# A Griffin-style decoder block on one Trainium2 core: one projection conversion, the bias conversions and one activation half moved

## What is computed

```python
def mixer(...):
    q, k, v, xr, yr, ga, gl = split_cols(h @ w_in)
    ...
    y_attn = sliding_window_attention(q, k, v, attn_sinks) @ w_attn_o
    ...
    y_lru = (rg_lru(...) * jax.nn.gelu(yr)) @ w_lru_o
    merged = jax.nn.sigmoid(ga) * y_attn + jax.nn.sigmoid(gl) * y_lru
    return merged @ w_out

def moe(...):
    logits = (t @ w_router + b_router).astype(jnp.float32)
    top_val, top_idx = lax.top_k(logits, TOP_K)
    gate = jax.nn.softmax(top_val, axis=-1)
    ...
    def expert_block(args):
        xc, e = args
        gu = xc @ w_gate_up[e] + b_gate_up[e]
        g, u = gu[:, :D_EXPERT], gu[:, D_EXPERT:]
        g = jnp.minimum(g, SWIGLU_LIMIT)
        u = jnp.clip(u, -SWIGLU_LIMIT, SWIGLU_LIMIT)
        act = (u + 1.0) * (g * jax.nn.sigmoid(SWIGLU_ALPHA * g))
        return act @ w_down[e] + b_down[e]
```

## Time and profile before

| | us |
|---|---|
| three runs | 2124.33, 2125.55, 2130.52 |
| median | 2125.55 |
| the profiled execution | 2121.84 |
| its span, first to last instruction | 2120.2 |
| mean granted TensorE clock | 0.972 of 2.4 GHz |

### The profile page before, as it was taken

The page is one execution under the profiler, slowest core; times in us unless marked ns, Lnnn a source line. Parts: engine busy times, 40 slices in busy tenths (PEclk is TensorE's granted clock), DMA queues, the critical chain, the costliest instruction groups (busy, mean ns, idle before and its releaser), DMA issues.

```text
span 2120.2 us, 37270 instructions
## 1 busy us (share of the span) xinstructions
PE 1987.3 (94%) x11800; PEld 1531.1 (72%) x11801; DVE 1572.9 (74%) x2031; ACT 1290.7 (61%) x1763; POOL 297.2 (14%) x335
## 2 busy tenths in 40 slices
PE   6999999999888699999999999999999999999992
PEld 5777777878666577777777777777777777777772
DVE  4778755555654788788777779977878988977894
ACT  5555455454523467667666667766667767756774
POOL 3100000000113402111222110221111101221100
PEclk9999999999998799999999999999999999999996
DMA  5020111011632969889888889978889979888994
GB/s 177 21 100 1 40 40 40 21 40 40 211 110 97 277 235 370 285 285 378 290 283 292 291 289 380 364 261 306 290 288 374 378 269 370 299 276 290 377 333 167
DMA packets 255968, 489.52 MB, mean 231 GB/s; under 512 B 20011, under 2 KB 38279, under 8 KB 255824
## 3 DMA queue, kind: packets, MB, share of 16 engines
q1 hardware_dynamic: 233824, 439.56, 57.6%
q0 software_dynamic: 21056, 49.34, 8.9%
q10 hardware_dynamic: 1040, 0.00, 0.0%
HBM read 461.01 MB, written 32.05 MB: 233 GB/s over the span
## 4 chain that ended last, share of the span: by engine, by line
PE 86%; DVE 6%; ACT 3%; issue 2%; SPq 1%; DMA 1%; DVEq 0%; POOLq 0%; ACTq 0%
PE psum L778 17%; PE psum L779 16%; PE psum L782 16%; PE psum L795 8%; PE psum L467 3%; PE psum L597 3%; PE psum L601 3%; PE psum L599 3%; PE psum L469 3%; PE psum L468 3%; PE psum L766 2%; PE psum L743 1%; PE psum L806 1%; PE psum L714 1%; PE psum L715 1%
## 5 line engine op out<-in xcount | busy, mean ns | idle before, releaser
L1779 DVE TENSOR_TENSOR w_lo<-ring,w_hi 128x1024 fp32r<-128x1024 f32 x768 | 910.3, 1221 | 125.7 <-ACT w_hi L1111 113.2
L1111 ACT ACTIVATE w_hi<-ring 128x1024 fp32r<-128x1024 f32 x768 | 795.8, 1057 | 227.1 <-PE psum L782 220.3
L778 PE MATMUL psum<-w_hi,rows_hi 128*128 128x512 f32 x1024 | 422.0, 412 | 8.1 <-DVE rows_lo L1783 5.6
L779 PE MATMUL psum<-w_hi,rows_lo 128*128 128x512 f32 x1024 | 399.8, 390 | 0.0
L782 PE MATMUL psum<-w_lo,rows_hi 128*128 128x512 f32 x1024 | 316.2, 390 | 0.0
L778 PEld LDWEIGHTS psum<-w_hi,rows_hi 128*128 128x128 f32 x1024 | 193.6, 189 | 51.1 <-issue 14.7
L782 PEld LDWEIGHTS psum<-w_lo,rows_hi 128*128 128x128 f32 x1024 | 192.5, 188 | 41.2
L779 PEld LDWEIGHTS psum<-w_hi,rows_lo 128*128 128x128 f32 x1024 | 193.2, 189 | 37.6
L778 PE MATMUL psum<-w_hi,act_hi 128*128 128x512 f32 x512 | 216.9, 424 | 1.9 <-issue 0.6
L779 PE MATMUL psum<-w_hi,act_lo 128*128 128x512 f32 x512 | 200.3, 391 | 0.3 <-issue 0.3
L795 PE MATMUL psum<-ring,region_m 128*32 128x256 f32 x3072 | 174.2, 380 | 0.0
(11 more groups left out here) (346 smaller groups left out, 2967.2 us busy)
## 6 DMA issues: line engine op xcount, KB each, us to landing
ring<-in_w_gate_up_dram SPq DMA_DIRECT2D x128, 2048.0 KB, 16.8
ring<-in_w_down_dram SPq DMA_DIRECT2D x64, 2048.0 KB, 15.0
ring<-in_w_in_dram SPq DMA_DIRECT2D x16, 512.0 KB, 5.2
region_m<-in_x_dram SPq DMA_DIRECT2D x8, 512.0 KB, 11.6
ring<-in_w_in_dram SPq DMA_DIRECT2D x2, 2048.0 KB, 17.5
ring<-in_w_out_dram SPq DMA_DIRECT2D x2, 2048.0 KB, 7.7
region_a<-in_x_dram POOLq DMA_DIRECT2D x8, 512.0 KB, 4.9
acc_rows<-region_a POOLq DMA_DIRECT2D x8, 512.0 KB, 2.9
```

The lines of the kernel that those rows point to most:

```text
L778: mm(bank(i), hi[:, ks], wh, start=(k0 + q == 0), stop=False)
L779: mm(bank(i), lo[:, ks], wh, start=False, stop=False)
L1111: act.activation(w_hi[:, n % NBUF, :], place[i][:, k0 * HALF:(k0 + 2) * HALF], ACT.Copy).then_inc(hi_done, 1)
L1779: v.tensor_tensor(out=w_lo[:, n % NBUF, :], in0=place[i][:, k0 * HALF:(k0 + 2) * HALF], in1=w_hi[:, n % NBUF, :].bitcast(f32), op=ALU.subt ...
```

## The change

Three independent moves:

- `out_high(16 * j + 3)` on ACT goes from behind the four sigmoids of block j to behind the first of them. PE no longer waits for all sigmoids ahead of a gate piece, but inside it, per q: for the two sigmoids of the banks that this q overwrites.
- `bias_part` on DVE goes from ahead of `top` to the end of the iteration, and is cut anew: seven parts in iterations 1 to 7 in place of five in 1 to 5. The subtraction over 96 partitions becomes two of half the columns; so does the one over 32 partitions. The copy of the third term goes to ACT, behind the last exponential. `bias_done` counts to 3.
- In the expert loop, `actT_out(1)` on ACT and `actT_low(1)` on DVE go from n = 20 to n = 19, ahead of the tail's sigmoid and of `tail_glu_part`, and so ahead of `high(20)` and `low(20)`.

```diff
--- before.py
+++ after.py
@@ -592,6 +592,8 @@
                     pe.wait_ge(score_read, 2 * NT)
                 pe.wait_ge(gate_lo, n + 1)
                 for q in range(2):
+                    if j >= 1 and k == 0:
+                        pe.wait_ge(sgate_done, 4 * j - 2 + 2 * q)
                     cols = slice(q * P, (q + 1) * P)
                     for th in range(2):
                         mm(gate_bank(th, q), hi[:, cols], hT_hi[:, k, th * HALF:(th + 1) * HALF], start=first, stop=False)
@@ -658,8 +660,6 @@
                 out_pieces(j, 0, LEAD)
                 done = LEAD
                 for k in range(KD):
-                    if k == 0:
-                        pe.wait_ge(sgate_done, 4 * (j + 1))
                     gate_piece((j + 1) * KD + k)
                     out_pieces(j, done, done + PER_GATE[k])
                     done += PER_GATE[k]
@@ -756,7 +756,7 @@
             last.then_inc(columns_mm, 1)
             pe.wait_ge(table_done, 1)
             total = pe.value_load(ends[0:1, 0:1], min_val=1, max_val=MAXS)
-            pe.wait_ge(bias_done, 1)
+            pe.wait_ge(bias_done, 3)
             BIAS_COL = (0, D, HALF, D + HALF, 2 * D, 2 * D + HALF)
             with pe.Fori(0, MAXS) as j:
                 with pe.If(j < total):
@@ -1007,6 +1007,8 @@
                 for q in range(2):
                     for th in range(2):
                         act.activation(sgate[th][q], bank(2 + 2 * th + q), ACT.Sigmoid).then_inc(sgate_done, 1)
+                        if q == 0 and th == 0:
+                            out_high(16 * j + 3)
 
             gate_high(6)
             weight_high(0)
@@ -1020,7 +1022,6 @@
                 if not last:
                     gate_high((j + 1) * KD)
                 sigmoids(j)
-                out_high(16 * j + 3)
                 if last:
                     for p_ in range(4, 16):
                         out_high(16 * j + p_)
@@ -1097,6 +1098,9 @@
             part_out(NT - 1)
             for t in range(NT - 3, NT):
                 gate_exp(t)
+            act.wait_ge(bias_done, 2)
+            act.activation(bias3[64:96, :], bstage[64:96, :], ACT.Copy).then_inc(bias_done, 1)
+            act.wait_ge(bias_done, 3)
 
 
             def rowsT_out():
@@ -1146,6 +1150,8 @@
                                 sigmoid(1)
                             if n == 16:
                                 actT_out(0)
+                            if n == 19:
+                                actT_out(1)
                             if n == 17:
                                 with act.If(tail > 0):
                                     wait_reg(act, trowsT_mm, before + 1)
@@ -1154,8 +1160,6 @@
                                 with act.If(tail > 0):
                                     wait_reg(act, tgate_mm, before + 2)
                                     act.activation(tail_sig, bank(1)[:, 0:QC], ACT.Sigmoid, scale=ALPHA).then_inc(tgsig_done, 1)
-                            if n == 20:
-                                actT_out(1)
                         with act.If(tail > 0):
                             wait_reg(act, tactT_mm, before + 1)
                             act.activation(actT_tail, bank(3)[:, 0:2 * P], ACT.Copy).then_inc(tactT_done, 1)
@@ -1554,16 +1558,16 @@
                     dve.wait_ge(bias_in, 96)
                     then(v.tensor_scalar(bstage[0:96, D:2 * D], bstage[0:96, D:2 * D], 1.0, None, ALU.add))
                     then(v.tensor_copy(bias3[0:96, :], bstage[0:96, :]))
-                if j == 1:
-                    then(v.tensor_tensor(out=bstage[0:96, :], in0=bstage[0:96, :], in1=bias3[0:96, :], op=ALU.subtract))
-                if j == 2:
-                    v.tensor_copy(bias3[32:64, :], bstage[32:64, :])
-                    then(v.tensor_copy(bias3[64:96, :], bstage[64:96, :]))
-                if j == 3:
-                    then(v.tensor_tensor(out=bstage[64:96, :], in0=bstage[64:96, :], in1=bias3[64:96, :], op=ALU.subtract))
-                if j == 4:
-                    v.tensor_copy(bias3[64:96, :], bstage[64:96, :]).then_inc(bias_done, 1)
-                    dve.wait_ge(bias_done, 1)
+                if j in (1, 2):
+                    cols = slice(3 * HALF * (j - 1), 3 * HALF * j)
+                    then(v.tensor_tensor(out=bstage[0:96, cols], in0=bstage[0:96, cols], in1=bias3[0:96, cols], op=ALU.subtract))
+                if j in (3, 4):
+                    rows = slice(32 * (j - 2), 32 * (j - 1))
+                    then(v.tensor_copy(bias3[rows, :], bstage[rows, :]))
+                if j in (5, 6):
+                    cols = slice(3 * HALF * (j - 5), 3 * HALF * (j - 4))
+                    v.tensor_tensor(out=bstage[64:96, cols], in0=bstage[64:96, cols], in1=bias3[64:96, cols],
+                                    op=ALU.subtract).then_inc(bias_done, 1)
 
             rope_kv(0)
             rope_q(0)
@@ -1699,12 +1703,12 @@
                                        op0=ALU.mult, op1=ALU.mult).then_inc(h2_done, 1)
                 if t + 2 < NT:
                     merged_low(t + 2)
-                if 1 <= t <= 5:
-                    bias_part(t - 1)
                 if t >= 2:
                     top(t - 2)
                 if t >= 3:
                     place_rows(t - 3)
+                if t >= 1:
+                    bias_part(t - 1)
             top(NT - 2)
             place_rows(NT - 3)
             v.tensor_scalar(first_row[:, :, 0], iota_t[:], iota_p, float(-FAR), ALU.add, ALU.add)
@@ -1833,10 +1837,9 @@
                             if n == 17:
                                 up_part(1)
                             if n == 19:
+                                actT_low(1)
                                 with dve.If(tail > 0):
                                     tail_glu_part()
-                            if n == 20:
-                                actT_low(1)
                         with dve.If(more > 0):
                             dve.wait_ge(rowsT_done, j + 2)
                             rows_low()
```

## The result

The changed kernel took **2094.59 us** (median of four runs, 2092.93 to 2095.47), the kernel before 2125.39 (2124.33 to 2130.52). The ratio is 0.9849, with a 95% interval from 0.9832 to 0.9867. The medians differ by 30.8 us; 32.8 were forecast. A second set of runs gave 2091.92 against 2122.72, ratio 0.9851 (0.9836 to 0.9866).

A forecast was written before the change was run, and what follows sets the result against it. TensorE, busy 94% of the span, was taken as the bound, so only its waits counted. Savings of 9.1 + 17.0 + 6.7 = 32.8 us off the 2125.55 us median gave 2092.8 us, range 2087 to 2103.

The forecast's parts named there:

- Part one, 9.1: Gate stage, fourth projection piece: converting behind the first sigmoid saves 1.25 us in seven blocks, 0.4 in the last.
- Part two, 17.0: Routing iterations: moving the bias conversions saves 17.0 us, about 10.5 of TensorE waiting and 6.5 of clock.
- the clock's share: Routing iterations: 6.5 us saved because matmuls behind the stalls no longer run partly at 1.2 GHz.
- The cover of the last part: Last bias part, 1.7 us, fits where DVE idles 2.38 us for ScalarE's exponentials: costs nothing, at most 1.7.
- The ScalarE copy: Third bias term, 32 x 3072, behind the last exponential: takes 3.2 us, costs nothing under the gathered rows' wait, 3.2 at worst.
- Part three, 6.7: Expert loop: second activation half converted sooner removes TensorE's late start of the transposes, 14 x 0.48 us.
- A spare of 0.4 us: Expert steps with a tail: piece 20's subtraction ends near 1047.5-1047.6, TensorE reads it at 1047.96; the tightest cover.
- that the clock does not come back: Routing: TensorE stays at the lower clock as often as now, only 10.5 of 17.0 us come: 2099.3; chance 0.08.
- that the late start is the branch's own: Expert loop: the branch itself delays the transposes, so converting the activation half sooner changes nothing: 2099.5; chance 0.08.
- that the tail steps pay: Expert loop, 16 tail steps: late piece 20 subtraction; 0.7 late gives 2097.6, 3.0 gives 2134.4; slower than before, chance 0.02.
- that the gate pieces are held: Gate stage: later sigmoids hold the gate pieces, giving back 4.6 us: 2097.4; shares chance 0.09 with lateness in tail steps.
- The chance of 0.03 for two rivals together: Two rivals at once, said to leave under 6.4 us of gain, which measurement cannot tell from no change; chance 0.03.

The follow-up runs named there:

- The filled waits: Kernel before plus 12 throwaway full-fp32 matmuls in TensorE's waits ahead of the router product: 2126.89 us, ratio 1.0006; with 12 added outside those waits, 1.0029.
- the moved wait: Kernel before with only TensorE's wait for the second activation half put behind the branch of the next rows' turn: 2118.92 us, ratio 0.9971.

## Why the prediction was right, step by step

**The sum** was 32.8 us off the median, and the medians fell by 30.8; by the ratio it is 32.1, from 28.3 to 35.7. The forecast of 2092.8 lies 1.8 under the 2094.59 measured.

**Part one, 9.1.** Right: 1.22 us in each of seven blocks and 0.3 in the last give 8.9, and the gate stages at equal first block give 8.9 to 9.1. The 0.1 that was to stay of PE's 1.35 idle is 0.09. In the last block the gain was a quarter of a full one (a third was assumed): a new wait of 1.0 us appeared there at piece 4, which stands behind the remaining sigmoids. The new `sgate` waits cost nothing, as costed: no wait of a gate piece for a sigmoid is in PE's list.

**Part two, 17.0.** Measured 17.6 between the first and the last `x2`; alone, it took 16.9 off the time. The two remaining waits are 0.34 to 0.38 instead of 0.45, and the clock came back in full. The filled waits put the clock's share, forecast as 6.5, at 6.0 in the profiles and 4.9 by the time. That price is not fixed, as the iteration at 1.00 behind a 2.60 us wait showed.

The cover of the last part held. DVE's wait for the exponentials was 2.38 us; the part of 1.75 took its place:

```profile
661.86 1.75 DVE L1569 TENSOR_TENSOR ring<-ring,region_s 32x1536 f32<-32x1536 f32 x1
...
665.83 0.16 DVE L1662 RECIPROCAL ring<-ring 128x1 f32<-128x1 f32 x1 [0.46 <-ACT ring L1072]
```

The ScalarE copy was costed at 3.2 by its neighbours' rows; it took

```profile
669.42 2.76 ACT L1102 ACTIVATE region_s<-ring 32x3072 bf16<-32x3072 f32 x1
```

since one instruction of 3072 columns pays the fixed part once: with 1.057 for 1024 columns, that part is about 0.2 us, an estimate from these two durations. VectorE's cast of that shape takes 1.75. The Trainium skill ("ScalarE: Activation LUTs", What ACT_TABLE_LOAD costs) gives 186 ns and 0.833 ns a column for an instruction with immediate scale and bias, an estimate of 2.75 us, with which the trace agrees. It ends at 672.18, and PE then waits for the gathered rows' DMA until 684.64. From the last `x2` to the row turn it is 31.20 us, and was 30.45. Nothing shows that this is the copy's doing: in the profiles of the eight kernels without such a copy it is 30.19 to 32.82, in those of the six with it 28.76 to 31.29.

**Part three, 6.7.** Measured 0.50 in each of 14 steps, 7.0, where 0.48 was forecast; the loop is 8.0 shorter. The rest is 0.4 in hundredths over the other periods and 0.7 behind the last row turn, where piece 20 of the last step, which has no rows to turn, started 0.52 late behind the same wait; the forecast had left that step out. Alone it gave 6.5. The wait's place was named rightly, and the kernel with the wait behind the branch shows it. Two points were off. A spare of 0.4 us was estimated in the tail steps; it is 0.67. From the start of `act_lo` to the end of the subtraction it is 0.61 + 1.23 + 1.22 = 3.06 us, where the forecast end (1047.5 to 1047.6) meant 3.3 to 3.4 and its terms as listed even 3.61, which would have left 0.12 to spare and not 0.4: the operations start before the ones ahead of them end (1022.85 against 1022.93), and the tail's three take 1.23 us together and not 1.7. And each microsecond beyond was to cost 16 us; the first 0.41 cost 9.25 in the loop, not 6.6.

**The 2.0 us that are missing** lie inside the interval, so no term is shown to be too large by them; in the profiles two of the terms were rather too small (17.0 for 17.6, 6.7 for 8.0). The median that was taken as the base lay 3.7 above the profile of before.

What moves one execution by as much can be read from the 14 profiles. From the first gate matmul to the first `x2` the eight kernels without part one took 302.2 us where the first gate block was short and 303.1 where it was long; the six with part one took 292.5 and 295.0 to 295.3. So part one is worth 9.6 or 7.9 us there, and like for like the three parts' savings add up to 35.2 or 33.5. The profiles of before (short) and after (long) are an unlike pair, and differ by 7.0. What adds to the first block is the first output tile behind PE's wait of 6.4 to 6.7 us: 13.4 us (short) or 12.8 (long) without part one, 12.9 or 13.8 with it, at mean granted clocks of 0.83, 0.87, 0.86 and 0.80. How often each case comes in unprofiled runs, no run here tells.

The rivals: that the clock does not come back (2099.3) is refuted by rows at 1.00, that the late start is the branch's own (2099.5) by the moved wait, that the tail steps pay by 0.67 us of spare, and that the gate pieces are held by the period of 33.07. The chance of 0.03 for two rivals together was tied to a gain under 6.4 us; but clock and branch together, at 2106, would have left 19.6, so that chance does not follow from the cases named.

## To carry to other kernels

Ask of every side job on a busy engine which of its neighbours is waited for, and put it behind that one; here the place was worth 17 us and the cutting nothing that could be measured. When TensorE is made to wait in the middle of a stream of matmuls, read the granted clock of the stretch and count the slow matmuls behind the wait as part of its price. And an unmet wait ahead of a branch can show as "issue": move the wait to see.

## What the runs showed of the hardware

Twelve matmuls added ahead of the expert loop, in either of the two places tried, brought an idle time of 4.8 to 4.9 us for "issue" in the first pass of the loop, and 43 brought 6.16; kernels with the same number of matmuls as before have none. One more 16 KB transfer of the instruction queue (28 for 27) came with it each time, and PE went on 1.6 to 1.7 us after it had landed. It hid a gain of 5 to 7 us completely, so an experiment that adds instructions needs a twin that adds them idly.

The first gate block took 26.5 us at a clock of 1.00 or 28.1 at 0.94, in executions of the same code.

A conversion late by 0.41 us cost a step 0.55 to 0.6.
